# Dilated attention values in quarters, and a gated bias added to the stream ahead of the first attention

## What is computed

```
first block, layer 0:
  a = rmsnorm(x) * (1 + scale) + shift
  att = differential attention(a, 256 context keys + 512 own keys)   4 heads, width 512
  hy  = gated long convolution(a)                                    width 512
  x = x + gate * ([att, hy] @ mix_w_out + mix_b_out)                 # gate * mix_b_out: the gated bias
  x = x + gate2 * squared_relu_mlp(...)
first block, layer 1: the same with a multiscale pool in place of att and hy; then a norm
second block:
  h = rmsnorm(x) * (1 + scale1) + shift1;  proj = h @ w_in
  y_mlstm = mlstm(...)                                               width 512
  y_attn  = dilated attention, 8 heads of 64, three window patterns  width 512
  x = x + gate1 * ([y_mlstm, y_attn] @ w_out)
  x = x + gate2 * expert_choice_ffn(...)                             16 experts, 8 pairs
```

## Time and profile before

| | |
|---|---|
| median of 3 runs | 2536.44 us |
| profiled execution, its own time | 2539.14 us |
| its span | 2537.3 us |
| mean granted TensorE clock | 0.966 |
| PE, DVE, ACT, POOL busy | 93%, 39%, 24%, 5% of the span |
| first attention | about 322 to 415 us |
| dilated attention | 1444 to 1524 us |
| expert stage | from about 1600 us to the end |

### The profile page before, as it was taken

One profiled execution on the slowest core, in us unless ns is written; L12 is line 12 of the kernel. 1 busy time (PEld: TensorE's weight loads), 2 busy tenths in 40 slices (PEclk: granted clock), 3 DMA queues, 4 the chain that ended last, 5 costly groups with the idle time before them and its releaser, 6 DMA issues.

```text
span 2537.3 us, 24160 instructions
## 1 busy us (share of the span) xinstructions
PE 2349.0 (93%) x10181; PEld 1407.2 (55%) x10181; DVE 1001.8 (39%) x1610; ACT 616.4 (24%) x1001; POOL 114.4 (5%) x120
## 2 busy tenths in 40 slices
PE   5999989899999999999999988989898998989888
PEld 2445544588888788888777647524242333323232
DVE  4555463466663566665666353211111110101001
ACT  2112153333223333233456464100000000000000
POOL 2000000000000000000221322000000000000000
PEclk8999988999999899999999998999999999999999
DMA  9312230355553155551221205699999999999997
GB/s 360 108 67 83 100 133 1 116 191 187 179 196 124 50 166 199 183 199 35 88 68 34 79 30 232 258 430 431 431 430 431 430 430 431 431 430 428 431 431 306
DMA packets 122386, 594.09 MB, mean 234 GB/s; under 512 B 10674, under 2 KB 12224, under 8 KB 96678
## 3 DMA queue, kind: packets, MB, share of 16 engines
q1 hardware_dynamic: 118850, 583.18, 57.9%
q0 software_dynamic: 3120, 9.24, 1.1%
q10 hardware_dynamic: 308, 0.13, 0.0%
HBM read 590.39 MB, written 2.14 MB: 234 GB/s over the span
## 4 chain that ended last, share of the span: by engine, by line
PE 77%; DMA 14%; DVE 6%; ACT 2%; issue 1%; POOL 0%; DVEq 0%; ACTq 0%; POOLq 0%
PE PS L1231 15%; PE PS L912 9%; PE PS L913 9%; PE PS L914 9%; PE PS L965 6%; PE PS L709 6%; PE PS L149 5%; PE PS L1248 3%; PE PS L1258 2%; PE PS L871 2%; DMA RING<-in_w_gate_dram 2%; DMA RB_a<-in_w_down_dram 2%; DMA RB_a<-in_w_gate_dram 2%; DMA RING<-in_w_down_dram 2%; PE PS L793 2%; DMA RING<-in_w_up_dram 2%
## 5 line engine op out<-in xcount | busy, mean ns | idle before, releaser
L1231 PE MATMUL PS<-RING,HID_e 128*64 128x512 f32 x592 | 206.4, 611 | 11.1 <-DMA RING<-in_w_gate_dram 5.9
L1231 PE MATMUL PS<-RB_a,HID_e 128*64 128x512 f32 x576 | 200.2, 606 | 9.0 <-DMA RB_a<-in_w_up_dram 5.4
L2578 DVE TENSOR_TENSOR TMP<-TMP,PS 128x512 f32<-128x512 f32 x32 | 19.8, 682 | 359.7 <-PE PS L1231 359.7
L1231 PE MATMUL PS<-HID_e 128*64 128x512 f32 x304 | 136.0, 595 | 5.0 <-DMA HID_e<-in_w_gate_dram 2.6
L1231 PE MATMUL PS<-XT,HID_e 128*64 128x512 f32 x288 | 130.4, 602 | 7.7 <-DMA XT<-in_w_up_dram 5.1
L1231 PE MATMUL PS<-AT_g,HID_e 128*64 128x512 f32 x288 | 132.0, 607 | 3.6 <-DMA AT_g<-in_w_gate_dram 2.6
L1787 ACT ACTIVATE HID_e<-PS,cmat 128x128 f32<-128x128 f32 x32 | 12.1, 456 | 486.7 <-PE PS L149 486.7
L1231 PEld LDWEIGHTS PS<-RING,HID_e 128*64 128x64 f32 x592 | 63.7, 140 | 101.2 <-issue 82.4
L2586 DVE TENSOR_TENSOR HID_e<-PS,HID_e 128x512 f32<-128x512 f32 x16 | 10.3, 686 | 270.9 <-PE PS L1248 270.9
L1248 PE MATMUL PS<-RING,HID_e 128*64 128x512 f32 x304 | 106.2, 619 | 11.4 <-DMA RING<-in_w_down_dram 11.4
L1248 PE MATMUL PS<-RB_a,HID_e 128*64 128x512 f32 x288 | 105.3, 621 | 10.6 <-DMA RB_a<-in_w_down_dram 10.6
(11 more groups left out here) (465 smaller groups left out, 4670.1 us busy)
## 6 DMA issues: line engine op xcount, KB each, us to landing
RING<-in_w_up_dram SPq DMA_DIRECT2D x19, 2048.0 KB, 18.7
RING<-in_w_down_dram SPq DMA_DIRECT2D x19, 2048.0 KB, 22.0
RING<-in_w_gate_dram SPq DMA_DIRECT2D x18, 2048.0 KB, 22.6
RB_a<-in_w_gate_dram SPq DMA_DIRECT2D x18, 2048.0 KB, 22.0
RB_a<-in_w_up_dram SPq DMA_DIRECT2D x18, 2048.0 KB, 17.9
RB_a<-in_w_down_dram SPq DMA_DIRECT2D x18, 2048.0 KB, 22.0
RING<-in_mlp_w_dram SPq DMA_DIRECT2D x32, 1024.0 KB, 5.5
RB_a<-in_mlp_w_dram SPq DMA_DIRECT2D x32, 1024.0 KB, 5.2
```

Source lines behind the costliest of these rows:

```text
L1231: last = pe.matmul(b[64 * d:64 * d + 64, :], xv_[:, k, 64 * d:64 * d + 64], wv, start=k == 0, stop=k == 7)
L2578: dve.tensor_tensor(q, q, banks.of("up", n, fg), ALU.mult).then_inc(*V_moe.up("act", n, fg))
```

## The change

It consists of these edits.

1. Dilated values in quarters. `pe_dil_values(hp, st)` now does a quarter: the product for one of the four key tiles (two matmuls) and one quarter of the spread (two). The quarters of pair hp run in the four steps of pair hp + 1. `PTs` gets a fourth buffer, at 6144, where `mixed(k)` for k < 4 stands; so head 3 waits for `G_out lo 3`, POOL's last read there.
2. Fixed banks in that stage: logits in 0 to 3, turns in 4 and 5, values in 6, spread in 7.
3. ACT's `spread(hp)` and DVE's `out(hp)` move from the first step of pair hp + 1 to the first step of pair hp + 2; `high(4)` and `high(5)` move to the second step of pairs 2 and 3, `high(6)` behind the loop. POOL's `pool_part(5, 4)` moves ahead of `pool_out2(6)`.
4. Part 5 of the projection: one group ahead of the last turn, one ahead of the last pair's values, six behind.
5. The gated bias is added to XT at the end of `dve_qkv`, ahead of the attention, and not in `dve_out1`; the squares wait for L2182 alone.
6. At the end of the first attention, `pe_att_values(3)` runs behind the first group of the projection, the sums behind the second, the spread behind the third.

```diff
-        PTs = Turns([H(o, hid=HID3) for o in (10240, 12288, 0)])
+        PTs = Turns([H(o, hid=HID3) for o in (10240, 12288, 0, 6144)])
...
+            pool_part(pool, w, 5, 4)
             pool_out2(pool, w, 6)
-            for k in (4, 5, 6):
-                pool_part(pool, w, 5, k)
+            pool_part(pool, w, 5, 5)
+            pool_part(pool, w, 5, 6)
...
-            pe_att_values(pe, w, 3)
 
         def pe_out1(pe, w):
...
             products(0, 0, bs[0], range(4, 8))
-            pe_att_sums(pe, w, 3)
+            pe_att_values(pe, w, 3)
             bs.append(open_bank(0, 1))
             products(0, 1, bs[1], range(4, 8))
+            pe_att_sums(pe, w, 3)
+            bs.append(open_bank(0, 2))
+            products(0, 2, bs[2], range(4, 8))
             for h in range(4):
                 pe_att_spread(pe, w, h)
-            for j in (2, 3):
-                bs.append(open_bank(0, j))
-                products(0, j, bs[j], range(4, 8))
+            bs.append(open_bank(0, 3))
+            products(0, 3, bs[3], range(4, 8))
...
-            bs = [banks.take(w, ("logits", s, c), (V_dil, "logit", s, c)) for c in range(2)]
+            bs = [banks.seat(w, 2 * (s % 2) + c, ("logits", s, c), (V_dil, "logit", s, c)) for c in range(2)]
...
-                b = banks.take(w, ("dturn", s, c), (S_dil, "turn", s, c))
+                b = banks.seat(w, 4 + c, ("dturn", s, c), (S_dil, "turn", s, c))
...
-        def pe_dil_values(pe, w, hp):
-            b = banks.take(w, ("dpv", hp), (V_dil, "out", hp))
+        def pe_dil_values(pe, w, hp, st):
+
+            if st:
+                b, b2 = banks.of("dpv", hp), banks.of("dspread", hp)
+            else:
+                b = banks.seat(w, 6, ("dpv", hp), (V_dil, "out", hp))
+                b2 = banks.seat(w, 7, ("dspread", hp), (S_dil, "spread", hp))
...
             for s in range(16):
                 if s < 14:
                     pe_dil_logits(pe, w, s + 2)
+                if s == 15:
+                    bs = pe_open(pe, w, 5, lambda j: ((V_out, "out2", j, 0),), (0, 1, 2, 3))
+                    pe_parts(pe, w, 5, bs, range(1), AL3, AH3, out2_fed)
                 pe_dil_turn(pe, w, s)
-                if s % 4 == 0 and s:
-                    pe_dil_values(pe, w, s // 4 - 1)
-                if s == 13:
-                    bs = pe_open(pe, w, 5, lambda j: ((V_out, "out2", j, 0),))
-                if s >= 13:
-                    pe_parts(pe, w, 5, bs, (s - 13,), AL3, AH3, out2_fed)
-            banks.i -= 4
-            pe_dil_values(pe, w, 3)
-            pe_parts(pe, w, 5, bs, range(3, 8), AL3, AH3, out2_fed)
+                if s > 3:
+                    pe_dil_values(pe, w, s // 4 - 1, s % 4)
+            pe_parts(pe, w, 5, bs, range(1, 2), AL3, AH3, out2_fed)
+            for st in range(4):
+                pe_dil_values(pe, w, 3, st)
+            pe_parts(pe, w, 5, bs, range(2, 8), AL3, AH3, out2_fed)
...
                         PTs.take(w, (h,), (T_dil, "pv", hp))
                         w.wait_ge(*V_ml.at("ho", 3, 2))
+                        if h == 3:
+                            w.wait_ge(*G_out.at("lo", 3))
...
-                if i == 0 and s:
-                    spread(hp - 1)
-                elif i == 2 and s > 4:
-                    high(3 + hp)
-                if s >= 14:
-                    act_part(act, w, 5, s - 10)
+                if i == 0 and hp > 1:
+                    spread(hp - 2)
+                elif i == 1 and hp > 1:
+                    high(2 + hp)
+            spread(2)
+            act_part(act, w, 5, 4)
+            high(6)
+            act_part(act, w, 5, 5)
...
             dve_ada_add(dve, w, 11)
+            dve.tensor_tensor(gbo, mod0[:, 16:24, 0], vc("mix_b_out", 0, 8), ALU.mult).then_inc(*V_out.up("gbo"))
+            w.wait_ge(*V_out.at("gbo"))
+            for jj in range(8):
+                dve.tensor_scalar(XT[:, jj, :], XT[:, jj, :], gbo[:, jj:jj + 1], None, ALU.add).then_inc(
+                    *V_out.up("bias", jj))
...
-                w.wait_ge(*V_out.at("out1", jj, 0))
-                dve.tensor_scalar(XT[:, jj, :], XT[:, jj, :], gbo[:, jj:jj + 1], None, ALU.add).then_inc(
-                    *V_out.up("out1", jj, 1))
...
-                if s % 4 == 0 and s:
-                    out(s // 4 - 1)
+                if s % 4 == 0 and s > 4:
+                    out(s // 4 - 2)
+            out(2)
             out(3)
```

More of the change, by code:

```diff
@@ L1106, in pe_dil_turn @@
                 transposes(pe, b, [lg[:, st * 128:(st + 1) * 128] for st in range(4)]).then_inc(*T_dil.up("turn", s, c))
-        def pe_dil_values(pe, w, hp):
-            b = banks.take(w, ("dpv", hp), (V_dil, "out", hp))
+        def pe_dil_values(pe, w, hp, st):
[4 more added lines that the diff above has]
+                b2 = banks.seat(w, 7, ("dspread", hp), (S_dil, "spread", hp))
             w.wait_ge(*S_dil.at("turn", 4 * hp + 3, 1))
             w.wait_ge(*S_ml.at("av", 3))
[L1112 to L1118, removed]
-            w.wait_ge(*V_dil.at("recip", 4 * hp + 3))
[L1120 to L1125, removed]
+            for c in range(2):
+                h = 2 * hp + c
+                last = pe.matmul(b[64 * c:64 * c + 64, :], av[:, st, h * 64:(h + 1) * 64], PTs.of(h)[:, st, :],
+                                 start=st == 0, stop=st == 3)
+            if st == 3:
+                last.then_inc(*T_dil.up("pv", hp))
+            w.wait_ge(*V_dil.at("recip", 4 * hp + 3))
+            for c in range(2):
+                last = pe.matmul(b2[64 * c:64 * c + 64, st * 128:(st + 1) * 128],
+                                 soft(4 * hp + st, 3)[:, c:c + 1].to_broadcast([128, 64]), ident[:, :],
+                                 start=True, stop=True)
+            if st == 3:
+                last.then_inc(*T_dil.up("spread", hp))
         def pe_dil_key_turn(pe, w, i):
@@ L1145, in pe_dilated @@
                 pe_dil_rows(pe, w, j)
-            banks.i = 0
             pe_dil_logits(pe, w, 0)
             pe_dil_rows(pe, w, 3)
-            banks.i = 2
             pe_dil_logits(pe, w, 1)
@@ L1153, in pe_dilated @@
                     pe_dil_logits(pe, w, s + 2)
+                if s == 15:
+                    bs = pe_open(pe, w, 5, lambda j: ((V_out, "out2", j, 0),), (0, 1, 2, 3))
+                    pe_parts(pe, w, 5, bs, range(1), AL3, AH3, out2_fed)
                 pe_dil_turn(pe, w, s)
-                if s % 4 == 0 and s:
-                    pe_dil_values(pe, w, s // 4 - 1)
-                if s == 13:
-                    bs = pe_open(pe, w, 5, lambda j: ((V_out, "out2", j, 0),))
-                if s >= 13:
-                    pe_parts(pe, w, 5, bs, (s - 13,), AL3, AH3, out2_fed)
-            banks.i -= 4
-            pe_dil_values(pe, w, 3)
-            pe_parts(pe, w, 5, bs, range(3, 8), AL3, AH3, out2_fed)
-            banks.i -= 2
-            bs = pe_open(pe, w, 6, lambda j: ((V_out, "out2", 4 + j, 0),))
+                if s > 3:
[4 more added lines that the diff above has]
+            pe_parts(pe, w, 5, bs, range(2, 8), AL3, AH3, out2_fed)
+            bs = pe_open(pe, w, 6, lambda j: ((V_out, "out2", 4 + j, 0),), (4, 5, 6, 7))
             pe_parts(pe, w, 6, bs, range(4), AL3, AH3, out2_fed)
-            rbs = [banks.take(w, ("router", i), (V_moe, "logits", i)) for i in range(4)]
+            rbs = [banks.seat(w, i, ("router", i), (V_moe, "logits", i)) for i in range(4)]
             pe_router(pe, w, rbs, range(4))
@@ L1835, in scalar_program @@
             act_split(act, w, 0, 1)
-            act_norm_root(act, w, 2, lambda k: XT[:, k, :], 512, lambda k: V_out.at("out1", k, 1))
+            act_norm_root(act, w, 2, lambda k: XT[:, k, :], 512, lambda k: V_out.at("out1", k, 0))
             act_norm_split(act, w, 2, ffns[0][0], g2s, mod0[:, 24:32, 0], V_out.at("g2s"))
@@ L2177, in dve_out1 @@
         def dve_out1(dve, w):
-            dve.tensor_tensor(gbo, mod0[:, 16:24, 0], vc("mix_b_out", 0, 8), ALU.mult).then_inc(*V_out.up("gbo"))
-            w.wait_ge(*V_out.at("gbo"))
             for jj in range(8):
                 w.wait_ge(*T_out.at("out1", jj // 4, jj % 4))
+                w.wait_ge(*V_out.at("bias", jj))
                 dve.scalar_tensor_tensor(out=XT[:, jj, :], in0=banks.of("out1", jj // 4, jj % 4),
```

## The result

The changed kernel takes 2547.63 us (median of 4 runs, 2543.43 to 2550.49) where the kernel before took 2536.11 beside it: ratio 1.0042, 95% interval 1.0030 to 1.0055, so 7.6 to 14 us more. Measured again in the experiments it was 1.0031 (1.0019 to 1.0043), 4.8 to 10.9 us more. It is slower. The forecast was 2542.6 in a range of 2537.0 to 2547.5; it had the sign and the places, and was some microseconds short. The first measurement lies at the upper end of the range: 2547.63 as it stands, and 2547.1 if its ratio is applied to the 2536.44 from which the forecast starts. The second measurement gives 2544.3 in the same way.

A forecast was written before the change was run, and what follows sets the result against it. DVE was taken as the chain inside dilated pairs, the end standing a fixed distance behind the expert stage's start. First attention +1.6 and dilated attention +4.6 gave +6.2 us on 2536.44: 2542.6, range 2537.0 to 2547.5.

The forecast's parts named there:

- The additions: First attention's start: gbo and eight bias additions on DVE put the first maximum 2.7 us later, with nothing covering it.
- The tail: End of the first attention: one addition leaves the last tile's path, so the square starts earlier, giving back 0.5 us.
- The clock at the attention's start: PE's slow stretch in the first attention's longer idle time: cost change taken as 0, from 0.6 less to 1.5 more.
- The fourth rival: Attention's start: additions cost less, as longer idle time shortens PE's slow stretch; 2 us less, 2540.5, chance 0.08.
- The projection: End of the first attention: the projection's first group fills PE's 0.83 us gap, gaining 0.6 us, bounds 0.4 and 0.83.
- The first new wait: Dilated attention: PE waits 3.0 us ahead of pair 1's first quarter until `out(0)` frees bank 6.
- The second new wait: Dilated attention: DVE waits 5.3 us at `logits(12)` for bias rows queued on POOL behind `high(4)`, bounds 3.5 and 9.
- The clock behind the waits: Dilated attention: 1.9 us for PE's slow clock after 1503.9 (1.4 to 3), 0.3 for slower step 8 to 9.
- The third: Rival: slow clock after 1503.9 and in the attention lasts longer, or rows land slowest; +3 to +5 more, 2546.5, chance 0.14.
- The second rival: Dilated borders: no wait beyond 1 us, -10 or so there, about -8 in all, 2528, chance 0.08.
- The first rival: Dilated borders: bias rows not late, only the 3.0 us waits for `out`; +0.7 in all, 2537.1, chance 0.17.
- The chain of bank 6: Dilated attention: exponentials of step 9, copies, spread, then `out(0)` free bank 6 at 1482.8; PE waits 3.0 us.

The follow-up runs named there:

- proj_alone: The kernel before with only the end of the first attention reordered, values of head 3 behind the projection's first group: ratio 1.0001, +0.3 us.
- rows_first: The changed kernel with the bias rows of heads 6 and 7 issued ahead of POOL's wait for `high(4)`: ratio 1.0024, stage 123.9 us.
- dilated_alone: The kernel before with the dilated attention's edits alone: ratio 1.0017, +4.3 us, stage 128.6 us.
- bias_back: The changed kernel with the gated bias additions ahead of the attention undone: ratio 1.0030, stage 127.6 us.
- no_waits: `rows_first`, with ACT copying the spread ahead of the exponentials and not behind the copies: ratio 0.9989, stage 113.5 us.

## Why the prediction held, and where it was short

**The additions.** Forecast: the maximum 2.7 us later. Measured: 3.43 - 0.75 = 2.68. This term was right to 0.1 us. The tail gives back 0.52 us, 0.5 forecast: the last tile's square starts 0.84 us behind DVE's L2193 and, before, 475.71 - 474.35 = 1.36 behind the same line. Timelines of DVE and ACT after, for the earlier trace rows, and of DVE before:

```profile
473.64 0.75 DVE L2193 SCALAR_TENSOR_TENSOR XT<-PS,MODC,XT 128x512 f32<-128x512 f32 x1 [5.52 <-PE PS L871]
```

```profile
474.48 0.63 ACT L1361 ACTIVATE TMP<-XT 128x512 f32<-128x512 f32 x1 [6.24 <-DVE XT L2193]
```

```profile
474.35 0.75 DVE L2182 SCALAR_TENSOR_TENSOR XT<-PS,MODC,XT 128x512 f32<-128x512 f32 x1 [5.00 <-PE PS L871]
```

**The clock at the attention's start.** Taken as 0. In the earlier trace rows it stood low until 6 us after PE's return. In the first profile after the change PE returns at 329.27 and the clock stays low for the next 6.6 us, which would make its price the same to a few tenths. In the second PE returns at 328.94 and the clock is still at 0.50 at 337. Windows of PE, two of `after` and one of `after_again`:

```profile
329.00:330.00 1.00, 0.73 (x3) 0.54 1.05 410
...
335.00:336.00 1.00, 1.00 (x5) 0.54 1.05 387
```

```profile
336.00:337.00 1.00, 1.00 (x3) 0.50 1.06 387
```

The thirteen profiles together tell more than the pair. No other edit lies ahead of the attention's third turn of a map (338.78 us in the kernel before). From the first scores to it, the seven profiles without the additions ahead take 14.6 to 16.7 us, 16.0 in the mean, and the six with them 18.8 to 20.2, 19.9 in the mean. The difference is 3.8 us (3.0 to 4.7), and 2.7 of it are the additions. So the longer idle time of PE (5.1 us in all six, 2.4 in all seven) costs some 1.2 us more of slow clock, a term that the prediction took as 0 with 1.5 as its bound. The fourth rival, that the longer idle time shortens the slow stretch, has the sign wrong. How much of the 1.2 us reaches the end is not shown, since the clock falls at other places behind it.

**The projection.** The gap is gone. The forecast of -0.6 is inside the interval of `proj_alone`, which can't tell it from nothing. So this term is not tested.

**The first new wait.** Forecast 3.0 us ahead of pair 1's first quarter, released by `out(0)`; measured 3.19. Counted from the second logits it came 0.35 us later than laid out.

**The second new wait.** Forecast: rows issued at 1489.9, landing 4.4, a wait of 5.3. Measured from the same point: issue 0.8 us later, landing 4.1, wait 3.90. DVE came to `logits(12)` 1.9 us later than laid out, since `logits(11)` waited 1.66 us for the turn of step 9 (L588), which stood behind PE's slow logits; so the wait was shorter, and its end came only 0.5 us late. The Trainium skill's rule on GpSimd's transfers ("SBUF — State Buffer", the box on the DVE that blocks a DMA in SBUF: two separate sides) can't be tested by it: DVE rested, and the landing was near the fastest, as that rule too would have it.

**The clock behind the waits: the term that was too small.** The prediction took 1.9 us for one slow stretch behind 1503.9, with 1.4 to 3 as bounds, and 0.3 for the slower steps behind the first wait. The rows of the changed kernel show 3.1 us behind the second wait and 1.7 behind the first. The third group of the projection was to end 82.1 us behind the second logits (1526.3 + 2.2 - 1446.42); it ends at 1532.4 - 1449.0 = 83.4. Some 0.5 of these 1.3 us stood already when pair 2's quarters began, the rest fell behind it. Of the stage's 5.8 us, 4.6 were forecast.

Behind the first wait all five profiles that have it lose 1.7 us of clock. In the changed kernel most of it vanishes in DVE's wait for the rows, which ends only 0.5 us late; without that wait, in `rows_first`, it counts whole. Behind the second wait the price differs between executions. With the same wait of 3.6 us, two profiles lose 3.1 us and two (`dilated_alone`, `bias_back`) 1.8. In these two the third group ends 82.2 and 82.0 us behind the second logits, as laid out. That is in part luck, since pair 2's quarters begin 0.5 us late there too, and the rest runs 0.5 us faster than laid out.

The price could have been read ahead of time. The prediction says that the earlier trace rows show the one slow stretch; the dilated attention of before had two more, 4 us long and 1.7 us dear, behind waits of 1.08 and 0.72 us (windows at 1474 and 1491 above).

**The rivals.** The third, the costly clock at 2546.5 with a chance of 0.14, is nearer to the first measurement than the forecast is, and its two signs came in part: the slow stretch behind 1503.9 and the one in the attention were longer, while the bias rows landed fast. The second measurement lies between the two. The second rival, no waits at the borders, is what `no_waits` builds: its stage is 8.0 us shorter than before, where the rival had some 10. The upper end of the range, which the first measurement touches, comes from this rival.

The first rival shows the same error larger. It had the rows in time and counted 1.5 us for two slow stretches, -0.9 in all for the dilated part. `rows_first` is this case: +2.4, 3.3 us off. Its two stretches cost 1.7 and 3.1, together 4.8, 3.3 more than counted. So the weight given to the two waits, "the larger" for the rows, was wrong in the total: the rows' wait is worth 3.4 to 5.8 us of the stage and the bank's two 8.0 to 10.4. The chain of bank 6 was seen, and the slow clock behind it priced at 0.3 in the forecast and 0.75 a time in the rival. The Trainium skill ("TensorE: Matmul & The Clock Gate", What's actually happening) says that activity releases the clock and idling gives it up; that agrees with `no_waits`, whose borders have no idle time and whose clock stays at 1.00 there. The fall behind the router's matmuls does not look like idling in the profile, where PE is busy throughout; what makes it is not shown.

**What stays open.** The whole was measured at +10.6 and +7.9 us. The stage accounts for 5.8, the additions for 2.2 and the clock behind them for some 1.2, together 9.2, and the projection's -0.6 is untested. What is left can't be told from the scatter of the stages ahead: one stretch that no edit touches took between 139 and 144 us, and the first attention between 147 and 155.

## What to carry to other kernels

A wait of PE costs its idle time and the slow stretch behind it; here 3.2 to 3.6 us of idle time brought 1.7 to 3.1 more, so price the pair, and twice where it returns. Look for that price in the trace of before: a stretch behind a short wait of the same stage shows it. Splitting work into the gaps of a bound engine gains nothing while what frees its buffer stands behind a copy on another in-order engine: moving that one copy ahead of the exponentials took 9.7 us off a stage that was 5.8 us too long. And a transfer issued from an engine's queue inherits every compute wait ahead of it: when a step is moved later, look for the issues behind it.

## What the runs showed of the hardware

The place where the granted clock falls differs between executions of one kernel: with the same instructions, four stretches of the first attention stood at 0.74, 0.83, 0.83 and 0.83 in one and at 0.83, 1.00, 1.00 and 0.91 in another, and that moved the stage from 146.8 to 154.4 us. A stretch chosen from one instruction to another inside the dilated stage repeated to 0.1 us in three kernels of the old order and in two executions of the changed kernel, while the two other kernels with the changed order were 0.3 and 1.3 us off.

The same wait does not always cost the same: behind an idle time of 3.6 us on PE the slow clock cost 3.1 us in two profiles and 1.8 in two. Behind the waits of 1.08 and 0.72 us in the kernel before it cost 1.7, as much as behind one of 3.19. And about the end of the router's first 32 matmuls the granted clock fell to 0.50 for 3 to 7 us in twelve of thirteen profiles, with PE busy throughout.
